# Summing the gathered down rows in 64x64 quarters, one prompt tile at a time, in a two-layer decoder step

## What is computed

```python
q = (xt @ w_query).astype(jnp.float32).reshape(n, PEER_HEADS, 2, PEER_DKEY // 2)
s = jnp.einsum('nhpd,pkd->nhpk', q, subkeys.astype(jnp.float32))
s1, i1 = lax.top_k(s[:, :, 0], PEER_TOPK)
s2, i2 = lax.top_k(s[:, :, 1], PEER_TOPK)
cand = (s1[..., :, None] + s2[..., None, :]).reshape(n, PEER_HEADS, PEER_TOPK * PEER_TOPK)
best, ic = lax.top_k(cand, PEER_TOPK)
...
up = jnp.take(w_up, ek, axis=0).astype(jnp.float32)
act = jax.nn.gelu(jnp.einsum('nd,nhkd->nhk', xk.astype(jnp.float32), up), approximate=False) * gk
down = jnp.take(w_down, ek, axis=0).astype(jnp.float32)
return jnp.einsum('nhk,nhkd->nd', act, down)
```

## Time and profile before

| | |
|---|---|
| median of 3 runs | 5060.1 us (5054.08 to 5062.49) |
| span of the profiled execution, first to last instruction | 5042.8 us |
| own time of the profiled execution | not recorded apart; the median lies 17.3 us above its span |
| PE, DVE, ACT, POOL busy | 87%, 63%, 24%, 32% of the span |
| DMA, mean over the span | 292 GB/s |
| expert part of layer 0, first gather to last dot | 1096 to 2683 us |
| expert part of layer 1 | 3530 to 5030 us |

### The profile page before, as it was taken

How to read it: one execution, slowest core, us unless ns; L and a number is a source line. 1 busy time by engine, 2 the same in 40 slices (tenths; PEclk the granted TensorE clock), 3 DMA queues, 4 the chain that set the end, 5 groups by cost and what they waited for, 6 DMA issues and landing times. The chain is left out here.

```text
span 5042.8 us, 49934 instructions
## 1 busy us (share of the span) xinstructions
PE 4367.6 (87%) x17024; PEld 2583.3 (51%) x17024; DVE 3163.9 (63%) x7441; ACT 1188.3 (24%) x2971; POOL 1621.6 (32%) x1418
## 2 busy tenths in 40 slices
PE   8899999999989877789999897799999987777555
PEld 6866677755444323334476776776544443232111
DVE  6523323247878789855556644432778788995776
ACT  2211211113323323221111223110333232332111
POOL 0412000014444444433330241100444444444554
PEclk9999999999999999999999999999999999999777
DMA  2223232329999999999993234441999999999998
GB/s 110 84 74 120 73 127 96 137 115 415 415 409 410 416 420 413 412 420 419 419 419 149 84 109 166 169 163 40 387 419 404 412 413 420 420 413 418 416 414 342
DMA packets 266368, 1472.42 MB, mean 292 GB/s; under 512 B 27009, under 2 KB 77953, under 8 KB 113601
## 3 DMA queue, kind: packets, MB, share of 16 engines
q0 software_dynamic: 176608, 1263.35, 61.4%
q1 hardware_dynamic: 79168, 198.75, 10.7%
q10 hardware_dynamic: 10336, 7.12, 0.5%
HBM read 1433.90 MB, written 55.34 MB: 295 GB/s over the span
## 5 line engine op out<-in xcount | busy, mean ns | idle before, releaser
L3036 PE MATMUL ps<-early,diag 128*128 128x512 f32 (+1 forms) x3464 | 1692.2, 634 | 416.8 <-ACT diag L2944 416.3
L2826 POOL DMA_INDIRECT early<-in_peer,ids x980 | 1148.4, 1172 | 1430.1 <-PE ps L3036 1257.6
L2868 DVE SCALAR_TENSOR_TENSOR early<-early,rows 128x1024 f32<-128x1024 f32 x980 | 1184.2, 1223 | 443.9 <-DMA early<-in_peer,ids 441.8
L3036 PEld LDWEIGHTS ps<-early,diag 128*128 128x128 f32 (+1 forms) x3464 | 647.8, 195 | 1370.6 <-ACT diag L2944 679.0
L2944 ACT ACTIVATE diag<-consts_sb,weight 128x128 f32<-128x128 f32 (+1 forms) x1010 | 354.3, 391 | 769.5 <-DVE weight L2880 754.0
L1335 PE MATMUL ps<-hT,gate_ring 128*128 128x288 f32 (+2 forms) x1728 | 465.0, 424 | 6.4 <-ACT gate_out L1347 3.4
L1335 PEld LDWEIGHTS ps<-hT,gate_ring 128*128 128x128 f32 x1728 | 319.7, 193 | 144.9 <-issue 34.6
L2933 ACT ACTIVATE gel<-dot 128x2 f32<-128x2 f32 x576 | 117.4, 204 | 1116.3 <-DVE early L2868 925.0
L3036 PE MATMUL ps<-late,diag 128*128 128x512 f32 (+1 forms) x432 | 228.5, 671 | 83.5 <-ACT diag L2944 82.7
L2966 PE MATMUL ps<-late 128*128 128x320 f32 (+2 forms) x1024 | 251.8, 399 | 0.0
L2826 POOL DMA_INDIRECT late<-in_peer,ids x136 | 164.6, 1211 | 199.2 <-PE ps L3036 163.5
(11 more groups left out here) (394 smaller groups left out, 5859.3 us busy)
## 6 DMA issues: line engine op xcount, KB each, us to landing
gate_ring<-in_in_gate POOLq DMA_DIRECT2D x48, 512.0 KB, 4.2
slot<-in_w_branch SPq DMA_DIRECT2D x16, 1152.0 KB, 5.2
ring<-in_in_delta SPq DMA_DIRECT2D x8, 2048.0 KB, 8.4
late<-in_peer_query SPq DMA_DIRECT2D x32, 512.0 KB, 7.9
early<-in_peer,ids POOLq DMA_INDIRECT x980, 15.5
slot<-gate_rows SPq DMA_DIRECT2D x16, 864.0 KB, 7.0
...
gate_ring<-in_in_gate SPq DMA_DIRECT2D x24, 512.0 KB, 10.8
```

The source lines that it names most:

```text
L2826: pool.indirect_dma_start(place(q), None, table_rows, bass.IndirectOffsetOnAxis(ap=ids[:, n, c:c + 1], axis=0)).then_inc(s.pair[PLACE[q]], 16)
L2868: nc.vector.scalar_tensor_tensor(out=up, in0=up, scalar=1.0, in1=rows[:, n, :], op0=ALU.mult, op1=ALU.mult, accum_out=dot[:, i % 2, k:k + ...
L3036: ins = nc.tensor.matmul(g.ps[0:r, 2 * (n % 2) + m, :], diag[:, (SUMMED[q] - 1) % DIAGS, 0:r], place(q)[:, D + m * 512:D + (m + 1) * 512], ...
```

## The change

- The two choices of a group are summed together by 64x64 products. The diagonal of a choice is kept as 128 x 64 (two 64-row diagonals on top of each other). For each half of the columns PE makes four products: rows 0 to 63 and rows 64 to 127 of choice 0 go to PSUM partitions 0 to 63, those of choice 1 to partitions 64 to 127, row halves in different banks. So a tile takes four banks, 0 to 3 or 4 to 7 (`SUM_BANK`). The sample tile's choices take the two column halves.
- x no longer goes through PSUM. After a tile's end DVE adds the four blocks of 64 x 1024 to x (`fold`); `add_x`, `copy_x`, `add_own` and the last product with the identity are gone, and PE sums every choice. The sample tile's two blocks are added in `last_vector`.
- Tiles are taken one after the other. Tile 1 starts on banks 4 to 7, so all queries and scores must be done within tile 0's 64 groups: two units in every 8 groups (`ASKED`), and four units instead of two before the first group (`FIRST_ASKED`). The ring of query weights has four places.
- ACT copies queries and scores one group later than PE makes them.
- In the first 64 groups 44 parts of routing are done (the rest of tile 0 and four heads of tile 1); the other 28 heads follow with 4 parts in every 4.4 groups, from group 64 to 186.
- Ten places are used up to gather 32, eight up to 154, ten after that. The next layer's projections start at group 209.

```diff
-BY_GROUP = [(n, h * TOPK + c) for n, h in HEADS[:(TILES - 1) * PH] for c in range(0, TOPK, GROUP)]
-BY_GROUP += [(TILES - 1, c) for c in range(0, COUNT[TILES - 1], GROUP)]
+HEADS = [(n, h) for n in range(TILES) for h in range(PH)]
+BY_GROUP = [(n, c) for n in range(TILES) for c in range(0, COUNT[n], GROUP)]
 ROUTE_AT = {}
+SECOND_EARLY = 4
 for _h in range(PH):
+    for _at, _head in ((0, (0, _h + 1)), (4, (1, _h // 2))):
+        if _head[1] < PH and (_at == 0 or _h % 2):
+            ROUTE_AT.update({_h * STEP + _at + k: _head + (k,) for k in range(4)})
+for _i, _head in enumerate(HEADS[PH + SECOND_EARLY:]):
+    ROUTE_AT.update({PH * STEP + 22 * _i // 5 + k: _head + (k,) for k in range(4)})
...
-EXTENDED = 244
-Q_RING = 3
+EXTENDED = 154
+Q_RING = 4
-ASKED = ((0, 2), (3, 4), (6, 9), (11, 13))
-FIRST_ASKED, REST_ASKED = ((3, 5), (5, 6), (8, 10), (12, 13)), (0, 2)
+FIRST_ASKED = (("query", 0, 0), ("query", 1, 0), ("scores", 0, 0), ("scores", 1, 0),
+               ("query", 2, 0), ("query", 3, 0), ("scores", 2, 0), ("scores", 3, 0))
+ASKED = {0: (("query", 0, 1),), 1: (("query", 1, 1),), 2: (("scores", 0, 1), ("query", 4, 0)), 3: (("query", 5, 0),),
+         4: (("scores", 1, 1),), 5: (("scores", 4, 0),), 6: (("scores", 5, 0),)}
-BEGIN, BEGUN = (8, 9, 7, 0, 1, 2, 3, 4, 5, 6), 90
+BEGIN, BEGUN = (8, 9, 7, 0, 1, 2, 3, 4, 5, 6), 32
...
+QUARTERS = ((0, 0), (1, 1), (0, 1), (1, 0))
+SUM_BANK = (0, 4, 0, 0, 0)
+FOLD_AT = {TILE_END[n] + (2 if n < 2 else 1): n for n in range(TILES - 1)}
...
+            def fold(n):
+                dve.wait_ge(s.downs_done, TILE_END[n] + 1)
+                for c in range(2):
+                    for r in range(2):
+                        half, b = slice(r * NS, (r + 1) * NS), SUM_BANK[n] + 2 * r
+                        to = g.x[half, n, :].rearrange("p (a c) -> p a c", a=2)
+                        last = nc.vector.tensor_tensor(to, to, g.ps[c * NS:(c + 1) * NS, b:b + 2, :], ALU.add)
...
-                if i:
-                    add_own(i - 1)
+                if i in FOLD_AT:
+                    fold(FOLD_AT[i])
...
-                for kind, u, a in asking[i]:
-                    if kind == "query":
-                        query(u, a)
-                    else:
-                        scores(u, a)
-                for done in range(TILES - 1):
-                    if i == TILE_END[done] + 4:
-                        copy_x(done)
+                if i:
+                    for kind, u, a in asking[i - 1]:
+                        ask(kind, u, a)
...
+            def sums(i, n, m):
+                for r, k in QUARTERS:
+                    q, half = i * GROUP + k, slice(r * NS, (r + 1) * NS)
+                    last = nc.tensor.matmul(g.ps[k * NS:(k + 1) * NS, SUM_BANK[n] + 2 * r + m, :], diag[half, q % DIAGS, :],
+                                            place(q)[half, D + m * 512:D + (m + 1) * 512], start=i == tile_group(n),
+                                            stop=i == TILE_END[n])
...
-                for k in range(GROUP):
-                    q = i * GROUP + k
-                    if q in BY_VECTOR:
-                        continue
-                    pe.wait_ge(s.diagonal, SUMMED[q])
-                    for m in range(2):
-                        ins = nc.tensor.matmul(g.ps[0:r, 2 * (n % 2) + m, :], diag[:, (SUMMED[q] - 1) % DIAGS, 0:r],
-                                               place(q)[:, D + m * 512:D + (m + 1) * 512], start=q == FIRST_SUM,
-                                               stop=n < LAST_TILE - 1 and c0 + k == COUNT[n] - 1)
-                    ins.then_inc(s.downs_done, 1)
+                pe.wait_ge(s.diagonal, (i + 1) * GROUP)
+                for m in range(2):
+                    last = sums(i, n, m) if n < LAST_TILE else sample_sums(i, n, m)
+                last.then_inc(s.downs_done, 1)
```

More of the change, by code:

```diff
@@ L2965, in query @@
                 for k in range(KT):
-                    last = nc.tensor.matmul(g.ps[:, 4 + i % 2, 0:c.stop - c.start], late.ring[:, u % Q_RING, k, :],
+                    last = nc.tensor.matmul(g.ps[:, 4 + i % 2, 0:c.stop - c.start], weights_of(u)[:, k, :],
                                             late.hT[:, k, c], start=k == 0, stop=k == KT - 1)
@@ L2997, in scores, with ask, sample_sums @@
                 last.then_inc(s.far_sums if a else s.pe_b, 1)
-            def add_x(n, first):
-                r = ROWS[n]
-                for m in range(2):
-                    last = nc.tensor.matmul(g.ps[0:r, 2 * (n % 2) + m, :], ident(g, r), g.x[0:r, n, m * 512:(m + 1) * 512],
-                                            start=first, stop=not first)
+            def ask(kind, u, a):
+                if kind == "query":
+                    query(u, a)
+                else:
+                    scores(u, a)
+            def sums(i, n, m):
[4 more added lines that the diff above has]
+                                            stop=i == TILE_END[n])
+                return last
+            def sample_sums(i, n, m):
+                for k in range(GROUP):
+                    q = i * GROUP + k
+                    last = nc.tensor.matmul(g.ps[k * NS:(k + 1) * NS, SUM_BANK[n] + m, :], diag[:, q % DIAGS, :],
+                                            place(q)[:, D + m * 512:D + (m + 1) * 512], start=i == tile_group(n),
+                                            stop=i == TILE_END[n])
                 return last
@@ L3009, in _ @@
             pe.wait_ge(s.hT_b, out.place(1) + 1)
-            query(0, 0)
-            query(1, 0)
+            for kind, u, a in FIRST_ASKED[:2]:
+                ask(kind, u, a)
             out.turn(pe, 3)
             pe.wait_ge(s.x_added, out.added(3))
-            scores(0, 0)
-            scores(1, 0)
+            for kind, u, a in FIRST_ASKED[2:4]:
+                ask(kind, u, a)
             pe.wait_ge(s.hT_a, TILES)
             pe.wait_ge(s.hT_b, TILES)
+            for kind, u, a in FIRST_ASKED[4:]:
+                ask(kind, u, a)
```

179 lines of the change are left out of this document (63 added, 116 removed).

## The result

The changed kernel took 5065.2 us, the kernel before 5054.1 (medians of 15 runs each): a ratio of **1.0025**, interval 1.0017 to 1.0033. The forecast was 5 us faster; it is 11 us slower by the medians. That 5065.2 us stands inside the forecast's outer range of 5036 to 5082 us is no success: the forecast counted from 5060.1 us, the median of three runs, and the change went the other way.

The account below looks back on a forecast made before the run. The prediction took the DMA's gathers to bound the expert parts. Its terms, -3 - 2 + 3 - 0.5 = -2.5 us a layer, -5 for two, gave 5055 us from 5060.1, range 5036 to 5082.

Parts of the forecast that it names:

- The folds: DVE's additions to x after a tile: queued gathers cover them; 1 us for the two meeting routing, between zero and 5.
- One sign of being wrong: After the start, a DMA share below 0.95 in any stretch of 50 us would show the forecast wrong.
- The start: Before the first sums: more queries on PE delay gather 10, DMA runs dry; +3 us a layer, +7 if uncovered.
- Routing: DVE's routing spread over 122 groups instead of 64 takes back 4 us; with the fold -3 us a layer.
- The "5 us": From 4212 to 4540 us, where every group has routing: DVE holds the gathers back by 5 us.
- The stretch of eight places: Groups with queries: PE's relief against twice the queries for a group; -2 us a layer, between +3 and -6.
- The products: PE's sums of a group: four quarters run together, 1.8 us less, off the path that sets the end; zero.
- The tail: Last sums to last square: 5.4 to 7.2 us against 6.8; -0.5 us, from -1.4 to +0.4.
- The slower one (5082): First 64 groups: paced queries starve the gathers at the start and at weight waits; +11 us a layer, chance 0.17.
- Switching widths: Layer 0's stretch with projections: at 0.5 us for a change of width PE binds; +47 us, 5107 us, chance 0.05.

Follow-up runs that it names:

- foldlate: The changed kernel with the fold of tile 0 moved to group 100 and that of tile 1 to group 151; ratio to the kernel before 1.0011.
- foldsplit: The changed kernel with the four additions of each early fold apart, tile 0 in groups 92 to 101, tile 1 in 151 to 157; ratio to before 1.0009.
- startdouble: The changed kernel with one half query multiplied twice, 3.6 us more on PE ahead of the first group's sums; ratio to the kernel before 1.0036.
- dense: The changed kernel with heads routed from group 64 on every 4 groups instead of every 4.4; ratio to the kernel before 1.0015.
- sumstwice: The changed kernel with each group's products of the four tiles done twice; ratio to the kernel before 1.0321.

## Why the prediction was wrong

- *The folds.* "A gather lands 11.7 us after its issue with eight places, of which its own bytes are 2.54, so the queue holds some 9 us." This is the step that failed. The times from issue to landing in the kernel before (min, median, max), for its first three gathers, into an empty queue, and from 3640 to 4040 us:

```profile
DMA to landing us min/median/max: 5.8/7.8/9.0
```

```profile
DMA to landing us min/median/max: 6.4/11.8/18.4
```

  An empty queue already takes 5.8 us, so the median gather has 6 us of cover and the least covered 0.6. I had read a median as a floor and a latency as a reserve. At the fold itself the cover was 2.2 us in layer 0 and 3.0 in layer 1, by an estimate from the changed kernel's issues and packets: without the 4.95 us the next gather would have gone out at about 1469.5 us, its first byte comes 1.6 us after the issue, and the DMA had bytes until about 1473.4. For the two early folds I took 1 us, between 0 and 5. With the first one away, groups 64 to 80 lost 3.9 and 6.6 us less (foldlate) or 5.8 and 5.5 (foldsplit); at the second, groups 128 to 144 lost 0.1 instead of 0.9 and 1.3. One sign of being wrong that the prediction names did come, a DMA share below 0.95 over 50 us: 0.94 from 1465 to 1515 us.
- *The start*, +3 forecast, +7 if not covered: 4.5 and 4.9. The mechanism held: gather 10 was forecast 33.4 us after the first gather and went out after 33.5, and startdouble moves the loss nearly us for us. I left out the second release, behind the second query (gather 12 at 39.9 us, 30.3 before); how much of the 1.5 and 1.9 us beyond the forecast is its doing isn't shown.
- *Routing*, -3 with one of it for the folds: no gain, a miss of 4 us a layer, about as large as the folds'. Groups 128 to 208 lose 1.1 and 1.8 us more than before. The "5 us" came from a count of gathers issued in a window; one more or less at its edge is 2.5 us. By bytes, groups 128 to 176 lost 2.0 and 0.4 us before, so there was little to win, and dense shows that spacing wins none. DVE did get freer, waiting 23 us for gathers from group 128 to 191 of layer 0 instead of 12, but no time came of it.
- *The stretch of eight places*, -2: about right. With the folds in covered pieces (foldsplit) groups 16 to 128 lose 7.0 and 8.8 us, before 9.0 and 9.9; where ten places stand now, in 80 to 128, 4.1 fell to 0.4, and where eight came early, in 16 to 64, it rose by 2.7 and 1.2.
- *The products* at zero: right where the work was before, and the clock fell as foreseen (0.71 to 0.75 in groups 64 to 208, before 0.96 to 1.00). What I missed is that the change spends what they save on the queries (sumstwice).
- *The tail*, -0.5: from the last sums to the last square 7.2 us, before 6.8; the upper end of the term.
- *The rivals.* The slower one (5082) had the start in it and put the rest on weight loads; the waits of PE for these add up to 3.2 us in layer 0's groups 16 to 64. The fold, in the sum with 1 us, is what should have been a rival. Switching widths binds nothing: the query behind the first quarters starts at 1127.00 us, 0.07 before their modelled end, and groups 208 to 287 of layer 0 lost 2 us more, not 47. The Trainium skill (TensorEngine Tiling (Array Packing), Key Properties) says that a change of tiling mode drains the engine; no row here shows a length for it.

So layer 1's 6.8 us are 4.9 at the start, 1.2 in groups 16 to 64, 6.2 with the fold, -3.7 behind it to 128, 1.8 to 208, -1.4 to 287 and -1.7 in the last group, 7.3, less 0.5 for 0.2 MB that don't move in it.
